# Compression with its weights moving, head pairs in the attention of the first block, gates with features on partitions

## What is computed

```
h = rms_norm(x); q, kv, g_logits, z_a, uv, z_b, merge_logits = split(h @ w_in)
kc, vc = compress(k_c), compress(v_c)         # 15 blocks of 32 positions, 4 groups
# compress: hid = silu(einsum('bnlgd,lde->bnge', blocks + pe, w1)); hid @ w2
gates = sigmoid(g_logits)                     # 3 branches x 16 heads
o_c = softmax(q kc - slope*distance) vc       # masked; branch "compressed"
o_s = softmax(q ks - slope*distance) vs       # branch "selected", causal here
o_w = softmax(q kw - slope*distance) vw       # branch "window", causal here
o_a = (g0*o_c + g1*o_s + g2*o_w) * silu(z_a)
merged = sig(m_a)*(o_a @ w_up_a) + sig(m_b)*(o_b @ w_up_b)
x = x + merged @ w_out; ...                   # then the second block
```

## Time and profile before

| what | value |
|---|---|
| median of 3 runs | 2569.5 us (2566.9 to 2571.2) |
| the profiled execution | 2570.0 us |
| its span | 2568.3 us |
| PE busy | 2413.3 us, 94% |
| DVE busy | 1579.9 us, 62% |
| ACT busy | 1072.0 us, 42% |
| POOL busy | 395.1 us, 15% |
| mean granted clock | 0.956 |
| DMA | 391.9 MB, 153 GB/s over the span |

### The profile page before, as it was taken

The page is one execution under the profiler, slowest core; times in us unless marked ns, Lnnn a source line. Parts: engine busy times, 40 slices in busy tenths (PEclk is TensorE's granted clock), DMA queues, the critical chain, the costliest instruction groups (busy, mean ns, idle before and its releaser), DMA issues.

```text
span 2568.3 us, 43659 instructions
## 1 busy us (share of the span) xinstructions
PE 2413.3 (94%) x18818; PEld 2306.2 (90%) x18818; DVE 1579.9 (62%) x2648; ACT 1072.0 (42%) x1433; POOL 395.1 (15%) x254
## 2 busy tenths in 40 slices
PE   2898999999999996999999899997899999999997
PEld 2898999999999995999999777797899999898997
DVE  3432555555456555439999888787665546666554
ACT  2322444554444343434334444443444434444442
POOL 1000000000000000028778200272000012221000
PEclk6887999999999998989999899998999999999998
DMA  4633444555555663445555344456455565555551
GB/s 140 166 105 89 126 142 137 163 154 179 182 164 181 187 191 100 148 121 176 168 169 180 100 139 128 137 165 176 139 172 179 166 186 145 162 164 149 176 185 66
DMA packets 409470, 391.93 MB, mean 153 GB/s; under 512 B 45464, under 2 KB 403160, under 8 KB 408954
## 3 DMA queue, kind: packets, MB, share of 16 engines
q1 hardware_dynamic: 373406, 381.69, 48.6%
q10 hardware_dynamic: 35872, 7.46, 1.6%
HBM read 386.77 MB, written 5.95 MB: 153 GB/s over the span
## 4 chain that ended last, share of the span: by engine, by line
PE 87%; DVE 7%; ACT 2%; ACTq 2%; DMA 1%; issue 1%; SPq 0%; DVEq 0%; PEldq 0%
PE ps L412 25%; PE ps L414 24%; PE ps L413 24%; PE ps L2111 3%; PE ps L2178 1%; DVE wlo L365 1%; PE ps L1953 1%; DMA raw<-in_w_in_dram 1%; DVE arena L1598 1%; DVE ps L1514 1%; PE ps L2155 1%; PE ps L2167 1%; PE ps L1886 1%; PE ps L1978 1%; PE ps L485 1%
## 5 line engine op out<-in xcount | busy, mean ns | idle before, releaser
L412 PE MATMUL ps<-op_hi,whi 128*128 128x256 f32 (+1 forms) x5440 | 1579.6, 290 | 44.5 <-DVE wlo L365 24.8
L414 PE MATMUL ps<-op_hi,wlo 128*128 128x256 f32 (+1 forms) x5440 | 1561.2, 287 | 0.0
L413 PE MATMUL ps<-op_lo,whi 128*128 128x256 f32 (+1 forms) x5440 | 1559.1, 287 | 0.0
L358 ACT ACTIVATE whi<-raw 128x1024 fp32r<-128x1024 f32 (+1 forms) x688 | 721.3, 1054 | 1052.5 <-PE ps L414 948.7
L412 PEld LDWEIGHTS ps<-op_hi,whi 128*128 128x128 f32 x5440 | 1038.5, 191 | 82.3 <-issue 72.8
L365 DVE TENSOR_TENSOR wlo<-raw,whi 128x1024 fp32r<-128x1024 f32 x560 | 678.0, 1227 | 614.1 <-ACT whi L358 613.6
L414 PEld LDWEIGHTS ps<-op_hi,wlo 128*128 128x128 f32 x5440 | 1038.1, 191 | 0.0
L413 PEld LDWEIGHTS ps<-op_lo,whi 128*128 128x128 f32 x5440 | 1036.9, 191 | 0.4 <-issue 0.2
L365 POOL TENSOR_TENSOR wlo<-raw,whi 128x1024 fp32r<-128x1024 f32 x128 | 312.2, 2441 | 1363.1 <-ACT whi L358 1363.1
L1514 DVE SCALAR_TENSOR_TENSOR ps<-arena,param_cols,ps 128x257 f32<-128x257 f32 (+6 forms) x448 | 183.0, 489 | 0.6
L748 POOL TENSOR_TENSOR arena<-arena 128x256 f32<-128x256 f32 x64 | 63.4, 1010 | 277.0 <-DMA arena<-bias_by_column 277.0
(11 more groups left out here) (284 smaller groups left out, 1552.0 us busy)
## 6 DMA issues: line engine op xcount, KB each, us to landing
raw<-in_e_w_in_dram SPq DMA_DIRECT2D x96, 1024.0 KB, 5.4
raw<-in_w_in_dram SPq DMA_DIRECT2D x84, 1024.0 KB, 5.2
raw<-in_o_w_in_dram SPq DMA_DIRECT2D x64, 1024.0 KB, 6.0
raw<-in_e_w_out_dram SPq DMA_DIRECT2D x32, 1024.0 KB, 5.4
raw<-in_w_out_dram SPq DMA_DIRECT2D x16, 1024.0 KB, 5.3
raw<-in_w_ple_gate_dram SPq DMA_DIRECT2D x16, 1024.0 KB, 5.3
raw<-in_o_w_out_dram SPq DMA_DIRECT2D x16, 1024.0 KB, 5.3
arena<-cum_rows SPq DMA_DIRECT2D x16, 544.0 KB, 6.1
```

What stands on the lines that cost most here:

```text
L358: nc.scalar.activation(half_view(whi[c % 2], c, n), half_view(raw[c % RING], c, n), ACT.Copy).then_inc(hi_ready, 1)
L412: nc.tensor.matmul(o, wh, xh, start=(i % cpp == 0 and k == 0), stop=False)
L413: nc.tensor.matmul(o, wh, xl, start=False, stop=False)
L414: mm = nc.tensor.matmul(o, wl, xh, start=False, stop=(i % cpp == cpp - 1 and k == 7))
```

## The change

- `hidden(j)` holds the 30 columns of KB and moves the 128 columns of W1[l], so the result has 30 rows; KB is laid out with l outermost. ScalarE's silu writes hidN with 30 partitions (L826 of the changed kernel), TensorE turns it after two more chunks (`hidden_turn`), and ScalarE copies it to hid (`hidden_copy`).
- The gate is done by `narrow`: 48 columns of gate weights held, 256 positions moving. The sigmoid writes GT with gates on partitions; TensorE turns it after the first kvw chunk and VectorE copies it to gates.
- The 16 transfers into VCB are issued by GpSimd, once `hid_summed` has reached 2, its two memsets are done and VCN is ready.
- A unit of the head loop is two heads, one query block and one branch, 128 or 256 keys. `attn_norm` multiplies the exponentials by one over their sum and by the gate before they are turned. The sums hold the values and move the turned exponentials; the unit of the branch "selected" begins its accumulation with VCB by PcT (the compressed branch), the unit of "window" ends it; VectorE's `attn_take` copies the result to OA after every second unit, features on partitions. L1926 and ScalarE's copies, ON and its transposes go.
- Semaphores v_ms, ya_ms, h3_ms become one (`factor_ms`), and so for the square roots.

```diff
 def hidden(j):
-    mm = T.matmul(ps[:, 4, 0:2 * NC].rearrange("p (a n) -> p a n", a=2), W1[j][:, l, :], KB[:, :, :, l],
+    mm = T.matmul(ps[0:2 * NC, 4, 0:P], KB[:, l].rearrange("p a n -> p (a n)"), W1[j][:, l, :],
+def hidden_turn(j):
+    pe.wait_ge(S("hid_silu"), j + 1)
+    T.transpose(ps[:, 4, 256:256 + 2 * NC], hidN[0:2 * NC, :], ident[0:2 * NC, 0:2 * NC]).then_inc(S("hid_turned"), 1)
 ...
-            stream_pe(pe, "qb")
+            stream_pe(pe, "qb", hi=2)
+            hidden_turn(0)
+            stream_pe(pe, "qb", lo=2)
 ...
+def narrow(pe, name, n, NT):
+    o = ps[0:n, 2 * (s.p0 % 2), 0:NT]
+    for t in range(DT):
+        nc.tensor.matmul(o, wh[:, t, :], xh, start=(t == 0), stop=False)
+        nc.tensor.matmul(o, wh[:, t, :], xl, start=False, stop=False)
+        mm = nc.tensor.matmul(o, wl[:, t, :], xh, start=False, stop=(t == DT - 1))
 ...
-            natural(pe, "gate", [(0, P), (P, P)], 3 * HEADS)
-            stream_pe(pe, "kvw", hi=3)
+            narrow(pe, "gate", 3 * HEADS, S1)
+            stream_pe(pe, "kvw", hi=1)
+            (gates turned: two transposes, gates_psum)
+            stream_pe(pe, "kvw", lo=1, hi=3)
 ...
             pe.wait_ge(S("pct_ready"), 1)
             pe.wait_ge(S("vcb_landed"), 16 * HEADS)
-            for qb in range(2):
-                for half in range(2):
-                    T.matmul(ps[:, 4 + 2 * qb + half, :], PcT[0:120, half, qb, :], VCB[0:120, half, :], start=True,
 ...
 ScalarE, after the gate's sigmoid:
-            for h in range(HEADS):
-                nc.scalar.dma_start(VCB[r:r + NC, h // 8, (h % 8) * HD:(h % 8 + 1) * HD], ...)
 GpSimd, before its side("qb"):
+            pool.wait_ge(S("hid_summed"), 2)
+            for half in range(2):
+                g.do(nc.gpsimd.memset(VCB[half], 0.0))
+            g.sync()
+            pool.wait_ge(S("vcn_ready"), 1)
+            for h in range(HEADS):
+                nc.gpsimd.dma_start(VCB[h // 8][r:r + NC, (h % 8) * HD:(h % 8 + 1) * HD], ...)
 ...
 a_scores(U):
+                i, qb, branch = U // 4, U % 4 // 2, U % 2
+                pe.wait_ge(S("a_biased"), U)
+                for h in range(2):
+                    o = HD * h
+                    mm = T.matmul(ps[:, 4 + h, 0:n], qkvT[o:o + HD, i, P * qb:P * qb + P], kt[:, 0:n], start=True, stop=True)
+a_sums(U):
+                pe.wait_ge(S("a_pt"), U + 1)
+                pe.wait_ge(S("a_acc"), U // 2)
+                if branch == 0:
+                    T.matmul(ps[:, 7, at:at + P], VCB[i // 4][0:120, ...], PcT[0:120, i // 4, qb, :], start=True, stop=False)
+                for k in range(qb + 1):
+                    for h in range(2):
+                        mm = T.matmul(ps[o:o + HD, 7, at:at + P], Vn[:, branch, k, HD * G:HD * G + HD], PTb[...],
+                                      start=False, stop=(branch == 1 and k == qb))
```

More of the change, by code:

```diff
@@ L1248, in _ @@
                     v.sync()
[L1249 removed]
+                    dve.wait_ge(S("gates_psum"), 1)
+                    v.do(V.tensor_copy(gates[:, :, :], ps[:, 4, 0:6 * HEADS].rearrange("p (a n) -> p a n", a=2)))
+                    v.sync()
+                    dve.sem_inc(S("gates_copied"), 1)
                     v.do(V.tensor_tensor(cco.rearrange("p (a h) -> p a h", a=2), cz.rearrange("p (a h) -> p a h", a=2),
@@ L1911, in _ @@
                         mm.then_inc(S("sc_psum"), 1)
-            natural(pe, "gate", [(0, P), (P, P)], 3 * HEADS)
-            stream_pe(pe, "kvw", hi=3)
+            narrow(pe, "gate", 3 * HEADS, S1)
+            stream_pe(pe, "kvw", hi=1)
+            pe.wait_ge(acc_free, ST["kvw"].p0)
+            for qb in range(2):
+                mm = T.transpose(ps[:, 4, 3 * HEADS * qb:3 * HEADS * (qb + 1)], GT[0:3 * HEADS, P * qb:P * qb + P],
+                                 ident[0:3 * HEADS, 0:3 * HEADS])
+            mm.then_inc(S("gates_psum"), 1)
+            stream_pe(pe, "kvw", lo=1, hi=3)
             pe.wait_ge(S("pc_norm"), 1)
@@ L1955, in a_scores @@
-                mm.then_inc(S("a_scores"), 1)
+                i, qb, branch = U // 4, U % 4 // 2, U % 2
+                G, n = i // 2, P * (qb + 1)
+                pe.wait_ge(S("kx_ready"), 2 if branch == 0 else 3 + G // 2)
+                if U == 0:
+                    pe.wait_ge(S("vn1_copied"), 2)
+                else:
+                    pe.wait_ge(S("a_biased"), U)
+                for h in range(2):
+                    o = HD * h
+                    kt = qkvT[o:o + HD, 12 + 4 * branch + G // 2, :] if G % 2 == h else KX[o:o + HD, 2 * branch + G // 2, :]
+                    mm = T.matmul(ps[:, 4 + h, 0:n], qkvT[o:o + HD, i, P * qb:P * qb + P], kt[:, 0:n], start=True, stop=True)
@@ new lines, in a_scores, with a_sums @@
+                mm.then_inc(S("a_scores"), 1)
+            def a_sums(U):
+                i, qb, branch = U // 4, U % 4 // 2, U % 2
+                G, at = i // 2, P * qb
+                pe.wait_ge(S("a_pt"), U + 1)
+                pe.wait_ge(S("a_acc"), U // 2)
+                if branch == 0:
+                    if U == 0:
+                        pe.wait_ge(S("pct_ready"), 1)
+                        pe.wait_ge(S("vcb_landed"), 16 * HEADS)
+                    T.matmul(ps[:, 7, at:at + P], VCB[i // 4][0:120, P * (i % 4):P * (i % 4) + P], PcT[0:120, i // 4, qb, :],
+                             start=True, stop=False)
+                for k in range(qb + 1):
+                    for h in range(2):
+                        o = HD * h
+                        mm = T.matmul(ps[o:o + HD, 7, at:at + P], Vn[:, branch, k, HD * G:HD * G + HD],
+                                      PTb[:, U % 2, P * (h * (qb + 1) + k):P * (h * (qb + 1) + k) + P],
+                                      start=False, stop=(branch == 1 and k == qb))
+                mm.then_inc(S("a_pv"), 1)
```

211 lines of the change are left out of this document (97 added, 114 removed).

## The result

| | median, us | runs |
|---|---|---|
| before | 2569.7 | 2566.9 to 2571.2 (4) |
| changed kernel | 2523.4 | 2520.7 to 2523.9 (4) |

What follows compares the result with a forecast made beforehand. TensorE was taken as the bound, on 87% of the chain. Savings 5.5, 6.2, 14.7, 9.6, 3.44, 1.75 and 11.2, less 0.6, 0.3 and 0.9, gave 50.6 us: 2570.0 to 2519.4, median 2519, range 2511 to 2537.

Steps and rivals of the forecast that it cites:

- two hidden layers: Compression's hidden products, with W1 moving: 7.1 us each in place of 8.70 and 11.08, saving 5.5 us.
- turns of hidden and gates, with restarts: Added transposes on TensorE: 0.6 us for the two of hidden and 0.3 for those of the gates, a cost.
- half-clock stream behind sparse work: Streams in compression begun before the clock rises: 15.8 us at half speed, 7.9 us lost, to be regained.
- the fall that stays: One clock fall kept for the scores against kc (L1908): 3.4 us of stream at half speed, costing 1.7 us.
- gate: Gate with features on partitions: 48 products of 256 columns take 5.9 us for 20.6, saving 14.7 us.
- wait for wlo: TensorE's wait behind the gate, caused by VCB transfers in ScalarE's queue, goes: 9.6 us saved.
- compressed branch: The four products L1926 go, merged into the head loop: 3.44 us saved.
- pairs and the loop's start: Head loop: pairs save 0.35 us in each of 32 units, 11.2 us, less 0.9 waiting for VectorE's additions.
- transposes of ON: The 16 transposes of ON (L2007) go: 1.75 us saved.
- Rival 1: GpSimd's VCB issues are slow, each held by one wlo instruction: 2.04 us each, 14.8 us wait, time 2534; chance 15%.
- rival 4: GpSimd's VCB descriptors starve behind VectorE while TensorE waits after kvw: 4.6 us an issue, time 2575; chance 2%.

Runs made afterwards that it cites:

- the profile without a fall: Changed kernel with each of GpSimd's 16 small transfers cut into three, 48 issues with the same bytes: 2530.8 us, ratio 0.9847.
- the hidden layer's first timing: Changed kernel with the hidden products again holding W1 and moving 30 columns, without the two turns, timed the first time: 2529.4 us, ratio 0.9842.
- the loads moved: Changed kernel with the twelve loads of the hidden products' weights issued by GpSimd instead of ScalarE: 2510.4 us, and 2509.7 when repeated.

## Why the prediction was right, and where it was off

The sum was 50.6 us, and 46.4 came. By parts, from the two chains:

| part | predicted | measured |
|---|---|---|
| two hidden layers | 5.5 | 5.6 |
| turns of hidden and gates, with restarts | -0.9 | -1.2 |
| half-clock stream behind sparse work | 7.9 | 7.3 |
| the fall that stays | -1.7 | -2.8 |
| gate | 14.7 | 14.7, the fall's share taken out |
| wait for wlo | 9.6 | 9.6 |
| compressed branch | 3.4 | 3.4 |
| *up to the first scores* | 38.5 | 36.5 |
| pairs and the loop's start | 10.3 | 9.7 |
| transposes of ON | 1.75 | 1.75 |
| the rest of the program | 0 | -0.8 |
| the profiled execution | 50.6 | 47.2 |

The restarts in the second row are the first product of a stream behind other work, 0.32 in place of 0.12 us. By its own sum the prediction should have put the first scores at 223.2 us, and not near 222 (261.7 - 38.5).

- **Hidden layer: right**, 7.10 us as the row of the same moving size in the earlier trace rows gave. That it is no cheaper than the old form at full clock the prediction did not see.
- **The clock: right in kind, the kept fall mis-sized.** I kept one fall, "as short as the shortest above", 1.7 us. It was 6.8 us long. Against the earlier trace rows it cost 1.05 us in the products of L1943 (4.88 for 3.83) and 1.74 in the gate (7.64 for 5.9), 2.8 in all; against the profile without a fall, 3.1. The bound beside it ("one twice as long", 3.4) held it. The step that failed is what was measured. The four numbers above it (3.2, 5.3, 2.9 and 4.4; the shortest is 2.9, not 3.4) are only the parts of the falls that reached into the streams. Whole, the shortest fall of before lasted from 126.0 to 132.8 us, 6.8, as long as the one that stayed: the clock is 1.00 in the window below and 0.50 in the next, the first line of the earlier trace rows. The first scores came at 225.1 and not at 223.2 for this reason for the most part (1.1 to 1.4 of 2.0 us).

```profile
124.00:126.00 2.00, 2.00 (x21) 1.00 0.73 199
```

- **Gate and wlo wait: right**, each shown by its own run (13.6 and 11.2 when undone). The four parts undone one at a time give back 13.6 + 11.2 + 9.4 + 10.3 = 44.5 us, which with the 5.2 of the compressed branch and its transposes, not undone, is 3 us more than the whole 46.4; with the 6.0 of the hidden layer's first timing in place of 9.4 it is the whole. They add up as far as the runs can tell.
- **GpSimd: right that there is no wait**, with more room than the 0.81 us taken. Rival 1 had two prices. Held by VectorE's wlo instruction, an issue would have been 2.04 us: the longest of 64 in two kernels was 0.72. With the Trainium skill's figure for a VectorE copy (SBUF — State Buffer, the box on VectorE blocking DMA) the estimate would have been 2551. The prediction carried it too far: under "Who interferes with whom" the same page says that its probe saw copies stall such transfers and `tensor_tensor` not, and wlo is a TENSOR_TENSOR. This case agrees: the issues that lay beside wlo instructions alone took 0.52 us, and two that lay beside VectorE's copies 0.57 and 0.61.
- **Pairs: right**, 0.35 us a unit, in four units from 233.54 to 262.81 (7.32 each, 7.67 in the earlier trace rows), and the run with both on one half gives all of it back. The whole loop saved 9.7, where 11.2 - 0.9 = 10.3 were forecast. The start is as predicted: the first two pairs of scores take 1.71 us (225.13 to 226.84), 0.8 of it the wait for VectorE's two additions, where they took 1.50 and without the wait would take 0.9. Added up over both chains, scores with this wait take 17.7 us for 27.0 (9.3 saved, 9.7 predicted), the sums with the compressed branch 18.9 for 19.7, and the stream between them is 0.3 longer. That is the missing 0.6: 0.4 in the scores and 0.3 in the stream, less 0.1 that the sums gave more.
- **The last 0.8 us** lie behind 612 us of before. The step L2022 of the earlier trace rows begins 48.0 us earlier now (532.38), the end 47.2. The waits for VectorE and ScalarE in the later parts differ by some tenths each. Profiles with the same work from the first scores on differ by 3 us there (the table above), so these two profiles cannot give the 0.8 a cause, and none is shown.
- **Slower than before (rival 4): out.** It needed 4.6 us an issue. Tripling the issues cost 7.5 us in time.

## What to carry to other kernels

Before trusting a count of operations, price a short step by what it does to the clock in it and behind it: the hidden layer costs the same in both forms at full clock, and its gain is the clock's. Measure a fall from where the clock drops, and not from where the next stream begins. When two engines' chains meet at a buffer, look for DMA issues in the queue of the engine that feeds the bottleneck: here 16 issues cost 10 us and 12 others 11 us, both hidden in a row that reads "PE waits for VectorE", and an idle GpSimd took them for nothing. Where two products use half of TensorE's rows each, put them on different halves and next to each other; that is the whole gain of a pair.

## What was not expected of the hardware

- An issue by GpSimd of a small transfer within SBUF took 0.52 us, with 15 rows or with 5, beside VectorE's subtractions at work (up to 0.61 beside its copies within SBUF), against 0.81 on ScalarE; from issue to landing 3.1 to 3.3 us against 1.9. Of a 512 KB load from HBM it took 1.1 to 1.3 us.
- The same TensorE instructions before it, and yet the clock fell near 185 us to 0.50 for 6.8 us in four profiles (five, if the one with the old gate behind it is counted) and not at all in one. It costs 3.1 us each time. This is as much as the runs of one kernel spread, but the two profiles of the changed kernel both have it, and what differs otherwise between profiles lies behind the first scores and ahead of the first hidden product. With the loads moved it lasted 3.4 us, twice, and cost 1.5.
- Two fp32 products of 256 columns on different halves of TensorE's rows took 0.63 us together and 1.06 on the same half, each figure with a start of 0.2 in it (two products of 128 columns took 0.42 and 0.64, so 128 columns more cost 0.21 and 0.42).
